# Hybrid decoder trunk: the 20 columns of dt and forget gate, made by token instead of by feature

## The chip, the cores and the metric

The kernel runs as one program on one core of a Trainium2 chip. The metric is the device time of an execution in microseconds (us); lower is better. The engines are PE (TensorE, matmuls; PEld are its weight loads), DVE (VectorE), ACT (ScalarE), POOL (GpSimd) and SP (SyncE, which here only issues DMAs).

## The reference

Two layers, each of three sub-layers on x of 256 tokens by 1024 features: a SwiGLU feed-forward, a token mixer, a second feed-forward. Each has RMS norms before and after and shift, scale and gate rows made from a conditioning vector. The mixer projects h (256x1024) by w_in into 13 pieces and runs four branches on them. Two narrow pieces matter here, 16 columns of dt and 4 of the forget gate:

```python
rq, rk, rv, rg, pu, sz, sxbc, sdt, fq, fk, fv, ff, gl = jnp.split(h @ w_in, points, axis=-1)
dt = jax.nn.softplus(sdt + dt_bias)            # (256, 16)
log_f = jax.nn.log_sigmoid(ff + b_forget)      # (256, 4)
```

dt and its cumulated decays feed the SSD scan, log_f the forgetting attention. Everything else stays as it was.

## The kernel before

**Precision.** Products are made in fp32r, TensorE's rounded 32-bit type. Each operand is split into a high part (the rounded value) and a low part (what is left), and three products are added up: hi x hi, hi x lo, lo x hi. HH and HL (`h_both`) are the two parts of h, by feature: feature on the partitions, 8 blocks k of 128 features, 256 tokens. WH and WL (`w_hi`, `w_lo`) are those of the weights.

**The stream of weight chunks.** All weights of the big products come as 512 KB chunks in one order over both layers, numbered g. SP loads chunk g into RAW, a ring of 8, once chunk g-8 is used up (`w_used`). ACT copies it into WH, a ring of 7 (`split_to`, L1348). DVE writes the difference into WL over the raw data (L1697); a few chunks of the mixer are split on POOL. PE waits for the low part (`weights`, L744) and multiplies. The order on each engine is written by hand: each engine walks over the chunk index c of the sub-layer, and actions are tied to values of c. DVE's walk is up to 4 chunks ahead of c with its splits, ACT's up to 5.

**The mixer's chunks.** The list MIX (L46) says: "fv" has chunks 0 to 3 (made at the boundary), "dtff" is chunk 4, "pu" 5 to 8, "xbc" 9 to 20, then fq, fk, sz and the gates and branches. Outputs of neighbouring entries go to bank pairs 0-1 and 2-3 of PSUM in turn, and the first chunk of an entry waits until the pair was read out: `freed` (L1257). "dtff" has pair 2-3, and so has the first "xbc" entry, chunk 9.

**The 20 columns.** Chunk 4 holds only 8 blocks of 128x20 weights, loaded as [128, 8, 20] (L650). ACT and DVE split its 160 columns as one flat row. PE makes the result by feature: for each k the weights' 20 columns are stationary and 256 tokens of h move (L1249 to L1253), three matmuls for each k, 24 in all, into 20 partitions of bank 2. ACT copies 20x256 values to ZF (L1537). Three chunks later, at c = 7, PE transposes them in two halves of 128 tokens to bank 3 (L1096 to L1100), and DVE at c = 8 reads them by token, adds the bias and makes z and |z| (L2102 to L2109). `z_ok` then frees the pair for chunk 9 and starts ACT's exp at c = 9. At c = 10 DVE makes softplus and the decays from it, which PE needs at c = 16.

Of the kernel before, what the change touches and what calls it, by code (L numbers as in the profile page):

```python
# [14 lines left out]
P = 128  # L15
D = 1024
# [301 lines left out]
def build(nc, x_d, c_d, w_ada, b_ada, norm_pre, norm_post, w_ffn_in, w_ffn_out, w_in, pool_w, w_ret_out, w_pool_out,  # L318
          w_ssm_out, w_fox_out, w_out, vecs_d, consts_d, out_d):
    with ExitStack() as ctx:  # L320
# [47 lines left out]
        EPS = SMALL[:, 16:17]  # L368
        DUMMY = SMALL[:, 17:18]
        _, dg_off = sb("rows_area", [P, TT, P])  # L370
        ZF = at("dt_by_feature", [P, T], F32, dg_off)
        AR = at("decay_rows", [P, T], F32R, dg_off)
        SEL, _ = sb("row_selector", [P, 20], F32R)
        RB = SMALL[:, 18:20]
# [73 lines left out]
        def quad(b):  # L448

            return PS[:, b:b + 2, :].rearrange("p b (h i) -> p (b h) i", h=2)  # L450

        def con(a, n):
            return KC[:, a:a + n]
# [76 lines left out]
        yph_ok = Signal(sem("y_pool_hi_ready"), 1)  # L530
        ypl_ok = Signal(sem("y_pool_lo_ready"), 1)
        pm_ok = Signal(sem("pool_weights_landed"), 16)
        zf_ok = Signal(sem("dt_by_feature_ready"), 1)
        zt_ps = Signal(sem("dt_by_token_in_psum"), 1)
        z_ok = Signal(sem("z_abs_ready"), 1)
        aexp_ok = Signal(sem("a_exp_ready"), 1)
        e_ok = Signal(sem("exp_abs_ready"), 1)
# [203 lines left out]
        def _(pe):  # L741
# [351 lines left out]

            def mixer_core(layer, c):

                if c == 7:  # L1096
                    pe.wait_ge(zf_ok.sem, zf_ok.at(layer, 1))
                    for tt in range(TT):
                        ins = pe.transpose(PS[:, 3, tt * 20:(tt + 1) * 20], ZF[0:20, tok(tt)], ident[0:20, 0:20])
                    ins.then_inc(zt_ps.sem, 1)  # L1100
                if c == 16:
                    if layer == 0:
                        pe.wait_ge(small_landed, 16 * N_SMALL)
# [127 lines left out]
            def mixer(s):  # L1231
                layer = s // 3
                first_tokens(s)

                acts = {"ret": (YRH, YRL, yrl_ok), "pool": (YPH, YPL, ypl_ok),
                        "ssm": (YSH, YSL, ysl_ok), "fox": (YFH, YFL, yfl_ok)}
                freed = [None, None]
                n_gate, n_mul, n_pool, n_sz, n_xbc = 0, 0, 0, 0, 0
                for i, (name, col, n, by_token) in enumerate(MIX):
                    if name == "fv":  # L1240
                        continue
                    pair = i % 2
                    for j in range(n):
                        c = MIX_AT[i] + j
                        g = BASE[s] + c
                        mixer_core(layer, c)
                        if name == "dtff":
                            wh, wl = weights(g)
                            for k in range(KD):  # L1249
                                cs = slice(20 * k, 20 * k + 20)  # L1250
                                mm(PS[0:20, 2, 0:T], wh[:, cs], HH[:, k, :], start=(k == 0), stop=False)
                                mm(PS[0:20, 2, 0:T], wh[:, cs], HL[:, k, :], start=False, stop=False)
                                ins = mm(PS[0:20, 2, 0:T], wl[:, cs], HH[:, k, :], start=False, stop=(k == KD - 1))  # L1253
                            ins.then_inc(w_used, 1)
                            freed[pair] = (z_ok, 1)
                            continue
                        if j == 0 and freed[pair] is not None:  # L1257
                            sig, count = freed[pair]
                            pe.wait_ge(sig.sem, sig.at(layer, count))
                        if by_token:  # L1260
                            hi, lo = HH, HL
                            if name in acts:
                                hi, lo, ready = acts[name]
                                if j == 0 and col == 0:
                                    pe.wait_ge(ready.sem, ready.at(layer, 1))
                            token_chunk(g, j, 2 * pair, hi, lo, 2 * n, (0, 1)).then_inc(w_used, 1)
                            continue
                        wh, wl = weights(g)
                        for kk in range(2):
                            k = 2 * j + kk  # L1270
                            for t in range(4):
                                out = PS[:, 2 * pair + t // 2, (t % 2) * T:(t % 2 + 1) * T]
                                cs = slice(kk * HALF + t * P, kk * HALF + (t + 1) * P)
                                mm(out, wh[:, cs], HH[:, k, :], start=(k == 0 and t % 2 == 0), stop=False)  # L1274
                                mm(out, wh[:, cs], HL[:, k, :], start=False, stop=False)  # L1275
                                ins = mm(out, wl[:, cs], HH[:, k, :], start=False, stop=(k == KD - 1 and t % 2 == 1))  # L1276
                        ins.then_inc(w_used, 1)
                    if name == "gate":
                        n_gate += 1
                        freed[pair] = (gate_ok, n_gate)  # L1280
                    elif name == "pool":
                        n_pool += 1
                        freed[pair] = (pooled_out, n_pool)
                    elif name in ("ssm", "fox", "ret"):
                        n_mul += 1
                        freed[pair] = (gmul_ok, n_mul)
                    elif name == "xbc":
                        n_xbc += 1
                        freed[pair] = (conv_ok, n_xbc)
                    elif name == "sz":  # L1290
                        n_sz += 1
                        freed[pair] = (sz_ok, n_sz)
                    elif name in ("rq", "rk"):
                        freed[pair] = (rcos_ok, 1 if name == "rq" else 2)
                    elif name != "dtff":
                        freed[pair] = ({"pu": pu_ok, "fq": fq_ok, "fk": fk_ok, "rv": rv_ok, "rg": rg_ok}[name], 1)

                def before(k):
                    mixer_core(layer, WOUT + k)
                    if k == 0 and s + 1 < SUBS:  # L1300
                        pe.wait_ge(sh_ok.sem, sh_ok.at(s, 1))
                    if k % 4 == 0:
                        pe.wait_ge(ml_ok.sem, ml_ok.at(layer, k // 4 + 1))

                out_chunks(s, WOUT, KD, YSH, YSL, before)
# [29 lines left out]
        def _(act):  # L1335
# [3 lines left out]
            def split_to(g):  # L1339

                while state["next"] <= min(g, CHUNKS - 1):
                    n = state["next"]
                    state["next"] += 1
                    act.wait_ge(landed[n % N_RAW], LANDED[n])
                    if n >= N_HI:
                        act.wait_ge(w_used, n - N_HI + 1)
                    width = KD * 20 if is_dtff(n) else D
                    fn(WH[:, n % N_HI, 0:width], RAW[:, n % N_RAW, 0:width], ACT.Copy).then_inc(w_hi, 1)  # L1348

            def done(g):  # L1350
                act.wait_ge(w_used, g)
# [168 lines left out]
            def mixer(s):  # L1520
                layer = s // 3
                n_gate, n_sz, n_xbc = 0, 0, 0
                for c in range(N_MIX - TAIL):
                    g = BASE[s] + c
                    ended = [i for i, m in enumerate(MIX) if MIX_AT[i] + m[2] == c]
                    if ended:
# [5 lines left out]
                        if name == "fv":  # L1532
                            done(g)
                            fn(FV[:], PS[:, 6:8, :], ACT.Copy).then_inc(fv_ok.sem, 1)
                        if name == "dtff":
                            done(g)
                            fn(ZF[0:20, :], PS[0:20, 2, 0:T], ACT.Copy).then_inc(zf_ok.sem, 1)  # L1537
                        if name in ("pu", "fq", "fk"):
                            done(g)
                            dst, sig = {"pu": (PU, pu_ok), "fq": (FQ, fq_ok), "fk": (FK, fk_ok)}[name]  # L1540
# [143 lines left out]
        def _(dve):  # L1684
# [3 lines left out]
            def split_to(g):  # L1688

                while state["next"] <= min(g, CHUNKS - 1):  # L1690
                    n = state["next"]
                    state["next"] += 1
                    if splits_on_pool(n):
                        continue
                    dve.wait_ge(w_hi, n + 1)
                    width = KD * 20 if is_dtff(n) else D
                    dve.tensor_tensor(WL[:, n % N_RAW, 0:width], RAW[:, n % N_RAW, 0:width], WH[:, n % N_HI, 0:width],  # L1697
                                      ALU.subtract).then_inc(w_lo, 1)

            def done(g):  # L1700
                dve.wait_ge(w_used, g)
# [345 lines left out]
            def mixer(s):  # L2047
# [3 lines left out]
                for c in range(N_MIX - TAIL):  # L2051
# [47 lines left out]
                        ada_step(t, i)  # L2099
                    if c == 3:  # L2100
                        gate_row(s)
                    if c == 8:  # L2102
                        dve.wait_ge(zt_ps.sem, zt_ps.at(layer, 1))
                        if layer == 0:
                            dve.wait_ge(small_landed, 16 * N_SMALL)
                        chain(dve.tensor_tensor(Z20[:], PS[:, 3, 0:40].rearrange("p (t n) -> p t n", t=2),
                                                vec(layer, V_B20, 20).unsqueeze(1).to_broadcast([P, 2, 20]), ALU.add))
                        chain(dve.tensor_scalar(Z20[:, :, 0:16], Z20[:, :, 0:16], -1.0, None, ALU.mult))
                        dve.scalar_tensor_tensor(E20[:], Z20[:], -1.0, Z20[:], ALU.mult, ALU.max).then_inc(z_ok.sem, 1)  # L2109
                    if c == 10:  # L2110
# [178 lines left out]
        def _(pool):  # L2289
            chain = Order(pool, pool_order)  # L2290

            def split(g):

                if g >= CHUNKS:
                    return
                pool.wait_ge(w_hi, g + 1)
                width = KD * 20 if is_dtff(g) else D
                pool.tensor_tensor(WL[:, g % N_RAW, 0:width], RAW[:, g % N_RAW, 0:width], WH[:, g % N_HI, 0:width],
                                   ALU.subtract).then_inc(w_lo_pool, 1)

            def zero(t, n):
                pool.memset(part(n), 0.0).then_inc(acc_zero.sem, 1)
# [87 lines left out]
```

## Time and profile before

| | us |
|---|---|
| median of 3 runs | 1488.42 (1487.47 to 1488.42) |
| profiled execution, device time | 1487.86 |
| its span, first to last instruction | 1485.8 |
| PE busy | 1473.5 (99%) |
| DVE busy | 1161.1 (78%) |
| ACT busy | 816.5 (55%) |

The span is what the trace covers; the device time is 2.06 us longer. Busy PE says that matmuls were in flight, which overlap: their durations (276 ns for 256 moving columns) are longer than the distance from one start to the next. The distances have to be read from a timeline or from the chain of waits. Times in the rows are us from the span's start unless they are means, which are ns.

### The profile page before, as it was taken

Reading aid. Unit: us, or ns where it says so; the run is one execution under the profiler, and the core shown is the slowest. Engines: PE = TensorE matmul, PEld = TensorE weight load, DVE = VectorE, ACT = ScalarE, POOL = GpSimd, SP = SyncE. Lnnn points to the kernel's source line nnn. Section 1 sums busy time; section 2 is a strip of 40 time slices with the busy share of each in tenths; the row PEclk is TensorE's granted clock in tenths of the full one; section 3 lists DMA queues with packets and bytes.
Section 4 is the critical chain, followed back from the end, with each engine's and each line's share of the span. In section 5 each row is a group of like instructions: output and inputs, shape, how many; then the busy total and the mean of one; then the engine's idle time right before and its main releaser. Section 6 shows DMA issues by size and latency. Waiting matters only on the chain.

```text
span 1485.8 us, 20504 instructions
## 1 busy us (share of the span) xinstructions
PE 1473.5 (99%) x7991; PEld 1259.6 (85%) x7991; DVE 1161.1 (78%) x1414; ACT 816.5 (55%) x1016; POOL 56.8 (4%) x56
## 2 busy tenths in 40 slices
PE   8999999999999999999999999999999999999998
PEld 5788889997988878888888888899888888888886
DVE  6888777867799878889787897776879988775663
ACT  4545465566563456556465564654746545664553
POOL 0000003200000000000000000050000000000000
PEclk9999999999999999999999999999999999999999
DMA  9899966556777847888768887665667787566652
GB/s 349 292 323 303 336 221 206 167 164 186 226 250 245 284 156 241 259 277 286 241 227 263 272 280 250 192 184 158 183 192 244 244 263 234 179 187 186 195 187 99
DMA packets 203623, 342.94 MB, mean 231 GB/s; under 512 B 18547, under 2 KB 118131, under 8 KB 203526
## 3 DMA queue, kind: packets, MB, share of 16 engines
q1 hardware_dynamic: 185382, 275.56, 58.2%
q10 hardware_dynamic: 18144, 66.07, 13.4%
q8 instruction: 63, 1.03, 0.3%
q14 instruction: 34, 0.28, 0.1%
HBM read 340.53 MB, written 1.05 MB: 230 GB/s over the span
## 4 chain that ended last, share of the span: by engine, by line
PE 97%; DVE 2%; ACT 1%; issue 1%; DMA 0%; DVEq 0%; ACTq 0%
PE ps L819 12%; PE ps L784 11%; PE ps L775 11%; PE ps L785 11%; PE ps L933 6%; PE ps L935 6%; PE ps L934 6%; PE ps L824 6%; PE ps L1274 5%; PE ps L1275 5%; PE ps L1276 5%; PE ps L867 3%; PE ps L973 1%; PE ps L860 1%; PE ps L1146 1%
## 5 line engine op out<-in xcount | busy, mean ns | idle before, releaser
L1697 DVE TENSOR_TENSOR w_lo<-w_raw,w_hi 128x1024 fp32r<-128x1024 f32 x480 | 574.7, 1219 | 100.7 <-ACT w_hi L1348 100.2
L1348 ACT ACTIVATE w_hi<-w_raw 128x1024 fp32r<-128x1024 f32 x490 | 504.7, 1051 | 259.5 <-DMA w_raw<-in_w_ffn_out 70.5
L784 PE MATMUL ps<-w_hi,h_both 128*128 128x512 f32 x586 | 231.0, 394 | 0.0
L785 PE MATMUL ps<-w_lo,h_both 128*128 128x512 f32 x586 | 228.3, 390 | 0.0
L775 PE MATMUL ps<-w_hi,h_both 128*128 128x512 f32 x586 | 227.6, 390 | 0.0
L819 PE MATMUL ps<-h_both,w_hi 128*128 128x512 f32 x768 | 206.6, 394 | 0.0
L1274 PE MATMUL ps<-h_both,w_hi 128*128 128x256 f32 x640 | 182.6, 285 | 0.0
L1276 PE MATMUL ps<-h_both,w_lo 128*128 128x256 f32 x640 | 181.1, 283 | 0.0
L1275 PE MATMUL ps<-h_both,w_hi 128*128 128x256 f32 x640 | 181.1, 283 | 0.0
L1713 DVE SCALAR_TENSOR_TENSOR ada_acc<-ada_slab,c_silu,ada_acc 128x1024 f32<-128x1024 f32 x128 | 163.7, 1279 | 5.7 <-DMA ada_slab<-in_w_ada 5.7
L819 PEld LDWEIGHTS ps<-h_both,w_hi 128*128 128x128 f32 x768 | 132.9, 189 | 19.2
L933 PE MATMUL ps<-w_hi,act_hi 128*128 128x512 f32 x352 | 137.6, 391 | 0.0
L935 PE MATMUL ps<-w_hi,act_lo 128*128 128x512 f32 x352 | 137.0, 389 | 0.0
L934 PE MATMUL ps<-w_lo,act_hi 128*128 128x512 f32 x352 | 137.0, 389 | 0.0
L784 PEld LDWEIGHTS ps<-w_hi,h_both 128*128 128x128 f32 x586 | 110.1, 188 | 24.1 <-DVE w_lo L1697 2.4
L775 PEld LDWEIGHTS ps<-w_hi,h_both 128*128 128x128 f32 x586 | 110.0, 188 | 23.4
L785 PEld LDWEIGHTS ps<-w_lo,h_both 128*128 128x128 f32 x586 | 110.2, 188 | 21.8
L824 PEld LDWEIGHTS ps<-h_both,w_lo 128*128 128x128 f32 x768 | 114.5, 189 | 14.2
L1274 PEld LDWEIGHTS ps<-h_both,w_hi 128*128 128x128 f32 x640 | 122.7, 192 | 0.6 <-issue 0.3
L1275 PEld LDWEIGHTS ps<-h_both,w_hi 128*128 128x128 f32 x640 | 122.8, 192 | 0.2
L1276 PEld LDWEIGHTS ps<-h_both,w_lo 128*128 128x128 f32 x640 | 122.7, 192 | 0.0
L824 PE MATMUL ps<-h_both,w_lo 128*128 128x256 f32 x768 | 118.3, 281 | 0.0
(310 smaller groups left out, 1860.2 us busy)
## 6 DMA issues: line engine op xcount, KB each, us to landing
w_raw<-in_w_ffn_in SPq DMA_DIRECT2D x352, 256.0 KB, 3.8
w_raw<-in_w_in SPq DMA_DIRECT2D x168, 512.0 KB, 3.7
ada_slab<-in_w_ada ACTq DMA_DIRECT2D x126, 512.0 KB, 4.6
w_raw<-in_w_ffn_out SPq DMA_DIRECT2D x88, 512.0 KB, 4.2
w_raw<-in_w_ssm_out SPq DMA_DIRECT2D x16, 512.0 KB, 4.7
w_raw<-in_w_out SPq DMA_DIRECT2D x16, 512.0 KB, 3.4
ada_slab_first<-in_w_ada SPq DMA_DIRECT2D x14, 512.0 KB, 7.2
w_raw<-in_w_pool_out SPq DMA_DIRECT2D x8, 512.0 KB, 3.6
```

The costliest lines, as they stand in the source:

```text
L775: return mm(PS[:, banks + tt, :], lo[:, k, tok(tt)], wh[:, kk * HALF:(kk + 1) * HALF], start=False, stop=(k == kn - 1))
L784: mm(out, hi[:, k, tok(tt)], wh[:, cs], start=(k == 0), stop=False)
L785: mm(out, hi[:, k, tok(tt)], wl[:, cs], start=False, stop=False)
L819: ins = mm(PS[:, bank, :], wh[:, cs], HB[:, k, :, :], start=(k == 0), stop=(k == KD - 1))
L824: ins = mm(PS[:, bank, 0:T], wl[:, cs], HH[:, k, :], start=False, stop=False)
L933: mm(out, hi[:, k, tok(tt)], wh[:, cs], start=first, stop=False)
L934: mm(out, hi[:, k, tok(tt)], wl[:, cs], start=False, stop=False)
L1274: mm(out, wh[:, cs], HH[:, k, :], start=(k == 0 and t % 2 == 0), stop=False)
L1275: mm(out, wh[:, cs], HL[:, k, :], start=False, stop=False)
L1276: ins = mm(out, wl[:, cs], HH[:, k, :], start=False, stop=(k == KD - 1 and t % 2 == 1))
L1348: fn(WH[:, n % N_HI, 0:width], RAW[:, n % N_RAW, 0:width], ACT.Copy).then_inc(w_hi, 1)
L1697: dve.tensor_tensor(WL[:, n % N_RAW, 0:width], RAW[:, n % N_RAW, 0:width], WH[:, n % N_HI, 0:width], ALU.subtract).then_inc(w_lo, 1)
```

## The change

h becomes the stationary operand and the weights move. For each half of 128 tokens and each k, the 128x128 tile of HH is loaded and the 40 columns [hi | lo] of the weights move through it; then the tile of HL is loaded and the 20 hi columns move. That makes 32 matmuls, and the result stands by token: for half tt, columns 64 tt to 64 tt + 19 of bank 2 hold the products with the hi weights, the next 20 those with the lo weights. The copy to ZF and the two transposes go. DVE reads at c = 7 (it waits for the chunk's last matmul), with one more add that joins the two groups of 20. The hi and lo weights stand side by side in one buffer of WH, in runs of 20 columns.

```diff
+        def dt_weights(g):
+            return WH[:, g % N_HI, 0:KD * 40].rearrange("p (k n) -> p k n", k=KD)
+        def dt_raw(g):
+            return RAW[:, g % N_RAW, 0:KD * 20].rearrange("p (k n) -> p k n", k=KD)
...
             def mixer_core(layer, c):
-                if c == 7:
-                    pe.wait_ge(zf_ok.sem, zf_ok.at(layer, 1))
-                    for tt in range(TT):
-                        ins = pe.transpose(PS[:, 3, tt * 20:(tt + 1) * 20], ZF[0:20, tok(tt)], ident[0:20, 0:20])
-                    ins.then_inc(zt_ps.sem, 1)
...
                         if name == "dtff":
-                            wh, wl = weights(g)
-                            for k in range(KD):
-                                cs = slice(20 * k, 20 * k + 20)
-                                mm(PS[0:20, 2, 0:T], wh[:, cs], HH[:, k, :], start=(k == 0), stop=False)
-                                mm(PS[0:20, 2, 0:T], wh[:, cs], HL[:, k, :], start=False, stop=False)
-                                ins = mm(PS[0:20, 2, 0:T], wl[:, cs], HH[:, k, :], start=False, stop=(k == KD - 1))
+                            weights(g)
+                            both = dt_weights(g)
+                            for tt in range(TT):
+                                for k in range(KD):
+                                    mm(PS[:, 2, tt * SHD:tt * SHD + 40], HH[:, k, tok(tt)], both[:, k, :],
+                                       start=(tt == 0 and k == 0), stop=False)
+                                    ins = mm(PS[:, 2, tt * SHD:tt * SHD + 20], HL[:, k, tok(tt)], both[:, k, 0:20], start=False,
+                                             stop=(tt == TT - 1 and k == KD - 1))
                             ins.then_inc(w_used, 1)
...
# ACT
-                    width = KD * 20 if is_dtff(n) else D
-                    fn(WH[:, n % N_HI, 0:width], RAW[:, n % N_RAW, 0:width], ACT.Copy).then_inc(w_hi, 1)
+                    if is_dtff(n):
+                        fn(dt_weights(n)[:, :, 0:20], dt_raw(n), ACT.Copy).then_inc(w_hi, 1)
+                        continue
+                    fn(WH[:, n % N_HI, :], RAW[:, n % N_RAW, :], ACT.Copy).then_inc(w_hi, 1)
...
-                        if name == "dtff":
-                            done(g)
-                            fn(ZF[0:20, :], PS[0:20, 2, 0:T], ACT.Copy).then_inc(zf_ok.sem, 1)
...
# DVE
+                    if is_dtff(n):
+                        dve.tensor_tensor(dt_weights(n)[:, :, 20:40], dt_raw(n), dt_weights(n)[:, :, 0:20], ALU.subtract)\
+                            .then_inc(w_lo, 1)
+                        continue
...
-                    if c == 8:
-                        dve.wait_ge(zt_ps.sem, zt_ps.at(layer, 1))
+                    if c == 7:
+                        done(BASE[s] + at_unit("dtff") + 1)
                         if layer == 0:
                             dve.wait_ge(small_landed, 16 * N_SMALL)
-                        chain(dve.tensor_tensor(Z20[:], PS[:, 3, 0:40].rearrange("p (t n) -> p t n", t=2),
-                                                vec(layer, V_B20, 20).unsqueeze(1).to_broadcast([P, 2, 20]), ALU.add))
+                        z = PS[:, 2, 0:2 * SHD].rearrange("p (t n) -> p t n", t=2)
+                        chain(dve.tensor_tensor(Z20[:], z[:, :, 0:20], vec(layer, V_B20, 20).unsqueeze(1).to_broadcast([P, 2, 20]),
+                                                ALU.add))
+                        chain(dve.tensor_tensor(Z20[:], z[:, :, 20:40], Z20[:], ALU.add))
                         chain(dve.tensor_scalar(Z20[:, :, 0:16], Z20[:, :, 0:16], -1.0, None, ALU.mult))
                         dve.scalar_tensor_tensor(E20[:], Z20[:], -1.0, Z20[:], ALU.mult, ALU.max).then_inc(z_ok.sem, 1)
```

## Rows read from the trace of the kernel before

**Rows 1.** The page: busy time by engine; the ended-last chain by engine.

```profile
PE 1473.5 (99%) x7991; PEld 1259.6 (85%) x7991; DVE 1161.1 (78%) x1414; ACT 816.5 (55%) x1016; POOL 56.8 (4%) x56
...
PE 97%; DVE 2%; ACT 1%; issue 1%; DMA 0%; DVEq 0%; ACTq 0%
```

**Rows 2.** Waits of PE (who waited for what: us in total, times, longest).

```profile
PE ps L1317 <- ACT c_silu L1668: 3.4, 1, 3.4
PE ps L984 <- DVE ada_acc_hi L1905: 1.8, 2, 0.9
PE ps L759 <- ACT h_both L1423: 0.5, 1, 0.5
PE ps L860 <- DVE act_full L1927: 0.3, 1, 0.3
```

**Rows 3.** Chain around the chunk: start us, us, what. Layer 1, then layer 0.

```profile
957.45 0.12 PE ps L1251
...
960.08 0.11 PE ps L1253
960.20 0.12 PE ps L1274
...
965.83 0.12 PE ps L1276
965.95 0.23 PE ps L1099 x2
966.18 0.32 PE ps L1274
...
231.21 0.12 PE ps L1251
...
233.96 0.12 PE ps L1274
...
239.59 0.12 PE ps L1276
239.71 0.23 PE ps L1099 x2
239.94 0.32 PE ps L1274
```

**Rows 4.** Timeline of weight loads: start us, us, engine, line (x: merged count).

```profile
413.06 0.64 PEld L1181 LDWEIGHTS ps<-small_columns,squares_ssd 128*128 128x128 f32 x4
413.62 0.19 PEld L784 LDWEIGHTS ps<-w_hi,h_both 128*128 128x128 f32 x1
...
266.55 0.30 PEld L1108 LDWEIGHTS ps<-da,consts 128*128 128x128 f32 x2 [0.17 <-issue]
266.76 0.30 PEld L1109 LDWEIGHTS ps<-da,consts 128*128 128x128 f32 x2
266.99 0.19 PEld L1274 LDWEIGHTS ps<-h_both,w_hi 128*128 128x128 f32 x1
...
337.54 0.53 PEld L1082 LDWEIGHTS ps<-decay_rows,row_selector 128*128 128x128 f32 x4 [0.17 <-issue]
```

**Rows 5.** The transposes: timeline of PE, then groups by form (busy, mean ns).

```profile
239.64 0.30 PE L1099 MATMUL ps<-consts,dt_by_feature 20*128 20x20 f32 x2
...
L1099 PE MATMUL ps<-consts,dt_by_feature 20*128 20x20 f32 x4 | 0.6, 222 | 0.0
```

**Rows 6.** Groups by form, DVE and ACT: busy us, mean ns of one.

```profile
L1697 DVE TENSOR_TENSOR w_lo<-w_raw,w_hi 128x160 fp32r<-128x160 f32 x2 | 0.6, 320 | 0.0
...
L1537 ACT ACTIVATE dt_by_feature<-ps 20x256 f32<-20x256 f32 x2 | 0.7, 364 | 0.3 <-PE ps L1253 0.3
L1348 ACT ACTIVATE w_hi<-w_raw 128x160 fp32r<-128x160 f32 x2 | 0.7, 330 | 0.0
```

**Rows 7.** Timeline of layer 1: start us, us, engine, line.

```profile
954.12 4.86 DVE L1697 TENSOR_TENSOR w_lo<-w_raw,w_hi 128x1024 fp32r<-128x1024 f32 x5
...
957.06 0.10 PEld L1251 LDWEIGHTS ps<-h_both,w_hi 128*20 128x20 f32 x1
...
960.02 3.49 DVE L1697 TENSOR_TENSOR w_lo<-w_raw,w_hi 128x1024 fp32r<-128x1024 f32 x3
...
964.12 1.23 DVE L1697 TENSOR_TENSOR w_lo<-w_raw,w_hi 128x1024 fp32r<-128x1024 f32 x1 [0.61 <-ACT w_hi L1348]
...
966.64 1.23 DVE L1697 TENSOR_TENSOR w_lo<-w_raw,w_hi 128x1024 fp32r<-128x1024 f32 x1 [1.30 <-ACT w_hi L1348]
```

**Rows 8.** Timeline of DVE, layer 0, with the z group.

```profile
233.80 4.80 DVE L1697 TENSOR_TENSOR w_lo<-w_raw,w_hi 128x1024 fp32r<-128x1024 f32 x4
239.79 1.23 DVE L1697 TENSOR_TENSOR w_lo<-w_raw,w_hi 128x1024 fp32r<-128x1024 f32 x1 [1.19 <-ACT w_hi L1348]
240.93 0.19 DVE L2106 TENSOR_TENSOR z<-ps,vectors 128x40 f32<-128x40 f32 x1
241.16 0.18 DVE L2108 TENSOR_SCALAR z<-z 128x32 f32<-128x32 f32 x1
241.37 0.20 DVE L2109 SCALAR_TENSOR_TENSOR e<-z 128x40 f32<-128x40 f32 x1
```

**Rows 9.** Start: chain; then windows of PE (busy, granted clock, DMA share, GB/s).

```profile
3.37 3.75 PE ps L1317 x4
7.12 3.71 PE ps L1312 x8
...
15.22 1.31 PE ps L1312 x6
...
0.00:15.00 15.00, 11.63 (x23) 1.00 0.91 299
...
957.00:960.20 3.20, 3.20 (x28) 1.00 1.00 323
```

**Rows 10.** Timeline of PE around the 16 transposes of XBC.

```profile
290.13 1.91 PE L1118 MATMUL ps<-consts,xbc 128*128 128x128 f32 x16
291.80 0.36 PE L1274 MATMUL ps<-h_both,w_hi 128*128 128x256 f32 x1
292.00 0.28 PE L1275 MATMUL ps<-h_both,w_hi 128*128 128x256 f32 x1
292.12 0.28 PE L1276 MATMUL ps<-h_both,w_lo 128*128 128x256 f32 x1
```

More of the change, by code:

```diff
@@ L370, in build @@
         _, dg_off = sb("rows_area", [P, TT, P])
-        ZF = at("dt_by_feature", [P, T], F32, dg_off)
         AR = at("decay_rows", [P, T], F32R, dg_off)
@@ L532, in build @@
         pm_ok = Signal(sem("pool_weights_landed"), 16)
-        zf_ok = Signal(sem("dt_by_feature_ready"), 1)
-        zt_ps = Signal(sem("dt_by_token_in_psum"), 1)
         z_ok = Signal(sem("z_abs_ready"), 1)
@@ L1695, in split_to @@
                     dve.wait_ge(w_hi, n + 1)
-                    width = KD * 20 if is_dtff(n) else D
-                    dve.tensor_tensor(WL[:, n % N_RAW, 0:width], RAW[:, n % N_RAW, 0:width], WH[:, n % N_HI, 0:width],
-                                      ALU.subtract).then_inc(w_lo, 1)
+                    if is_dtff(n):
+                        dve.tensor_tensor(dt_weights(n)[:, :, 20:40], dt_raw(n), dt_weights(n)[:, :, 0:20], ALU.subtract)\
+                            .then_inc(w_lo, 1)
+                        continue
+                    dve.tensor_tensor(WL[:, n % N_RAW, :], RAW[:, n % N_RAW, :], WH[:, n % N_HI, :], ALU.subtract)\
+                        .then_inc(w_lo, 1)
             def done(g):
@@ L2296, in split @@
                 pool.wait_ge(w_hi, g + 1)
-                width = KD * 20 if is_dtff(g) else D
-                pool.tensor_tensor(WL[:, g % N_RAW, 0:width], RAW[:, g % N_RAW, 0:width], WH[:, g % N_HI, 0:width],
-                                   ALU.subtract).then_inc(w_lo_pool, 1)
+                pool.tensor_tensor(WL[:, g % N_RAW, :], RAW[:, g % N_RAW, :], WH[:, g % N_HI, :], ALU.subtract)\
+                    .then_inc(w_lo_pool, 1)
             def zero(t, n):
```

## The prediction

> **What bounds the kernel now.** I read the page first. TensorE (PE) is busy for 1473.5 of 1485.8 us, and 97% of the chain that ended last is PE [rows 1]. The waits of PE's own instructions come next: apart from one wait of 3.4 us at the very start they are 1.8, 0.5 and 0.3 us in the whole run [rows 2]. So each us that PE issues more or less moves the end by a us, and what VectorE (DVE), ScalarE (ACT) and the DMA queue do counts only if PE begins to wait for it. Then the chain of waits around the 20-column chunk, once per layer (at 231 us and at 957 us). It is PE alone: 24 matmuls of the chunk, then the chunks of "pu", with two transposes three chunks later [rows 3]. The change touches these two stretches of PE and little else.
>
> **What goes from PE.** The 24 matmuls of a layer (L1251 to L1253, 20 stationary columns, 256 moving) run from 957.45 to 960.20, which is 2.75 us, 115 ns each; in layer 0 from 231.21 to 233.96, also 2.75 us [rows 3]. The two transposes at L1099 and the matmul behind them last from 965.95 to 966.50 (0.23 + 0.32), where a matmul of this stream takes 0.12. They cost 0.43 us; in layer 0, from 239.71 to 240.25, 0.42 us [rows 3]. Together 3.17 us per layer.
>
> **What comes to PE.** Two token halves by eight k give 16 pairs: a 128x128 stationary tile of h hi with 40 moving columns, and one of h lo with 20. That is 32 weight loads of 128 columns and only 960 moving columns, where 6,144 moved before. The moving columns can hardly be the price: at the 115 ns of 256 columns [rows 3] 40 of them are 18 ns. The load is. No row has a rounded (fp32r) matmul with under 256 moving columns, so I take the price from loads that stand close together. Four loads of 128x128 with one moving column (L1181): the first is issued at 413.06 under the matmul before; their group lasts 0.64, so the last began at 413.51, and the next line's load at 413.62, 0.11 later [rows 4]. Two with 20 moving columns at L1108 start at 266.55, two at L1109 at 266.76, and the next line's load at 266.99: 0.44 us for four, 110 ns each [rows 4]. Four rounded loads with a broadcast stationary (L1082): (0.53 - 0.19) / 3 = 113 ns [rows 4]. I take 110 ns: 32 x 0.110 = 3.52 us.
>
> Upwards: with 256 moving columns beside a full load the pace is 120 ns (960.20 to 965.95, 48 matmuls) [rows 3]; that gives 3.84 us. Further up, if a load did not run beside the matmul before it, 110 ns and the moving columns would add, 18 and 9 ns at the rate above: 32 x 0.1235 = 3.95 us. Furthest, if short rounded matmuls took as long as 256 columns and the loads added to that: 32 x (0.115 + 0.110) = 7.2 us; I give that end little, since every stream in the rows overlaps the two. Downwards: the two transposes of 20 columns with a quick load (their busy times 0.30 together, 0.222 for one) follow each other after 80 ns [rows 5]; 32 x 0.08 = 2.56 us. Two short loads or a load of another mode are no load of 128 rounded columns, so 110 is the nearer.
>
> Whether load and matmul overlap can be read: at the 120 ns pace [rows 3] there is no room for a full load of 110 ns and 256 moving columns one after the other. The Trainium skill speaks against the change here. "TensorE: Matmul & The Clock Gate", section "Part 3: Packing small matmuls", says that a load overlaps running matmuls only when they use other row groups; by it 128 full rows make load and matmul serial, 3.95 us per layer. The trace disagrees with its pace of 120 ns, and the trace decides.
>
> **PE's sum.** Per layer +3.52 - 2.75 - 0.42 = +0.35 us; two layers +0.70 us. Bounds: -1.22 us with the 80 ns pace (2.56 - 3.17 = -0.61 per layer), +1.34 with 120 ns, +1.56 with serial loads, +8.1 at the far end.
>
> **The waits.** PE's chunk still waits for the low part. The two copies and subtractions of 160 columns, now written in runs of 20 into one buffer, took 330 and 320 ns [rows 6]; the DVE group with it began at 954.12, behind one full subtraction of 1.22 it ends about 955.7, and PE's first load of the chunk starts at 957.06 [rows 7]. 1.4 us of slack cover a strided access even at double time. The first user of the other bank pair (the first "xbc" chunk, which waits for z_ok) begins after four "pu" chunks of 24 matmuls, 2.9 us each: about 972 in layer 1, and z_ok comes near 966.
>
> DVE gets one more 40-column add (about 0.19 us) and the group of z moves ahead of the subtraction of chunk 12. It is four instructions instead of three, 0.64 us from the first's start to the last's end, and 0.23 more for the new one: 0.87 us [rows 8]. In layer 1 chunk 11's subtraction ends at 965.35 and chunk 12's starts at 966.64, when ACT's copy is there: 1.29 us of idle time, of which 0.87 are used. In layer 0 the four subtractions end at 238.60 and the next starts at 239.79: 1.19 us [rows 7, 8]. The new wait in front (for the chunk's last matmul, about 961 and 235) is then long over; behind it is only chunk 12, which PE reads some 15 us later. Without that cover the price would be 0.87 us of DVE, not of PE. ACT loses a copy of 0.36 us [rows 6] and the stop before it; SP asks for chunk 12 some 0.77 us later, because the dt chunk is used up later, and PE is as late itself. All of that I put at nothing, and between -0.3 and +0.3 us.
>
> **From the sum to the time.** The profiled execution took 1487.86 us for its span of 1485.8. Plus 0.70 it would be 1488.56. The median of the runs shown, 1488.42, lies 0.56 above the profiled one, and the runs lie between 1487.47 and 1488.42; on the median the change makes 1489.1 us, which is what I predict.
>
> **The rivals.**
>
> 1. The loads come quicker than 110 ns. PE has only 20 or 40 columns between them, and the quickest neighbours in the trace are 80 ns apart [rows 5]. For it: less than a fifth of the moving columns. Against it: the three groups at 110 and 113 ns, one of them with a single moving column [rows 4]. It gives -1.22 us: 1487.2. The Trainium skill's page on TensorE, section "Back-to-back issue gap", has about 81 ns for a sustained stream with 128 columns; by that figure as an estimate the new block would be 2.6 us.
>
> 2. The load is not hidden, or a short rounded matmul has a floor of its own: +1.3 to +1.6 us from the two upper prices, 1489.7 to 1490.0, and in its tail up to +8.1, 1496.5. Against it stands the single-column group again.
>
> 3. The clock, which is the case on the slower side. The new block is the longest stretch in which the array mostly waits for loads, 3.5 us with 960 columns. At the start of the kernel 8 matmuls of 512 columns took 3.71 us (464 ns each, the pace of the 1.2 GHz level, though the granted clock is given as 1.00), and 6 of them later 1.31 us (218 ns, 2.4 GHz); PE had waited 3.4 us before [rows 2, 9]. If PE fell back to that pace after the new block, the same stretch would lose 3.71 - 8 x 0.218 = 2.0 us per layer, and if the four matmuls ahead of it (3.75 us) were slowed by half too, up to 3.9 us. Total +0.70 + 4.0 to 7.8: 1493.1 to 1496.9. It decides from 1.1 us lost per layer on. Against it: 16 transposes of 128x128 from 290.13 to 291.80 are followed by matmuls 0.12 us apart [rows 10], and the granted clock is 1.00 in every stretch [rows 9]. The same page of the Trainium skill, section "Part 1: The HAM clock gate", says that the clock is granted by how busy the array has lately been; by it a thin stream is a risk. No row has 3.5 us of such a stream.
>
> **Chances.** The forecast (load pace near 110 ns, PE's sum passed to the end) 0.72; rival 1 0.13; rival 2 0.09, a fifth of it beyond 0.2%; rival 3 0.03; unknown effects of moved instructions and buffers 0.03. About 0.2%, 3.0 us, is what a measurement here can tell from no change: 1485.4 to 1491.4. The forecast, rival 1 and most of rival 2 lie within; so 0.03 faster, 0.91 same, 0.06 slower. The range goes from rival 1 less the scatter of the runs (about 1 us) to rival 2 with it: 1486.2 to 1491.2.
>
> **What would show it.** Right: the 32 loads of the new block 107 to 115 ns apart; the block about 3.5 us from its first matmul to the first of "pu"; an even 0.12 us pace at chunk 7, where the transposes were; DVE's z group between chunks 11 and 12 with no wait in front; the "pu" matmuls at 0.12 us right after the block. Wrong: loads 80 ns apart or less (rival 1); over 120 ns (rival 2); "pu" matmuls at over 0.2 us behind the block (rival 3); a wait of PE for z or for the low part of the weights, or a change of more than 3 us elsewhere.

## The result and the profile after

| | before | changed |
|---|---|---|
| median, us | 1488.42 | 1491.91 |
| fastest and slowest of 17 runs | 1487.47 to 1489.34 | 1488.78 to 1495.72 |
| profiled execution, device time | 1487.86 | 1494.78 |
| its span | 1485.8 | 1492.8 |

The ratio is 1.0023, 95% interval 1.0016 to 1.0029: slower, by 3.5 us in the median. The forecast was 1489.1 with a range that ended at 1491.2. The spread is part of the result. The runs of before lie within 1.9 us, those of the changed kernel within 6.9. Each run also comes with the mean clock granted to TensorE over its span: the 7 runs of 1488.78 to 1489.98 have 0.999 or 1.000, the 10 of 1491.64 to 1495.72 have 0.995 to 0.998.

The page of the changed kernel, to be read against [rows 1]:

```profile
PE 1479.3 (99%) x8003; PEld 1265.5 (85%) x8003; DVE 1161.5 (78%) x1416; ACT 815.4 (55%) x1014; POOL 56.8 (4%) x56
```

PE is busy 5.8 us longer, for 12 matmuls more. Its own waits (us in total, times, longest) are 7.1 us, where those of [rows 2] are 6.0:

```profile
PE ps L1319 <- ACT c_silu L1669: 3.3, 1, 3.3
PE ps L989 <- DVE ada_acc_hi L1909: 2.5, 3, 0.9
PE ps L764 <- ACT h_both L1427: 0.5, 1, 0.5
...
PE ps L978 <- DVE y_tok L1849: 0.3, 1, 0.3
```

Three short waits are new. Those of L1013 (0.16 us, at 14.1) and the third of L989 (0.78 us, at 173.7) lie ahead of the first new block, and no other profile has them. That of L978 (0.26 us, at 1306.4) is in the profile of every kernel that starts from the changed one (their transposes of `y_tok`, under other line numbers), and not in those of before, e4 and e6; what brings it is not shown. Most of the 7.0 us of span is something else: PE became slower while it was busy. The windows of PE around the two blocks show where (stretch in us, its length, PE busy and matmuls, granted clock, DMA share, GB/s):

```profile
232.20:235.30 3.10, 3.10 (x30) 1.00 1.01 305
235.30:242.10 6.80, 6.80 (x34) 0.51 0.58 202
242.10:252.00 9.90, 9.90 (x84) 0.99 0.70 192
...
961.90:965.80 3.90, 3.90 (x36) 1.00 0.99 321
965.80:969.30 3.50, 3.50 (x19) 0.51 0.86 296
969.30:980.00 10.70, 10.70 (x91) 1.00 0.64 178
```

In both layers the clock is at 1.00 (2.4 GHz) through all or most of the new block and then at half, 1.2 GHz, for 6.8 us in layer 0 and 3.5 us in layer 1. I call that a fall. The chain of waits shows where it sets in and the pace, for layer 0 and then layer 1 (start us, us, what; L1252 has 40 moving columns, L1254 has 20, L1276 to L1278 are the "pu" matmuls that stood at L1274 to L1276 before):

```profile
232.43 0.02 PE ps L1252
...
232.56 0.12 PE ps L1252
232.68 0.10 PE ps L1254
...
235.46 0.18 PE ps L1252
235.64 0.20 PE ps L1254
235.84 0.23 PE ps L1252
236.08 0.20 PE ps L1254
236.27 0.41 PE ps L1276
236.68 0.21 PE ps L1277
...
242.02 0.21 PE ps L1278
242.23 0.16 PE ps L1276
242.39 0.12 PE ps L1277
...
962.18 0.02 PE ps L1252
...
965.65 0.22 PE ps L1276
...
966.02 0.21 PE ps L1278
...
969.41 0.12 PE ps L1276
```

In layer 0 the block begins at 232.43 and its last four matmuls, from 235.46 on, are slow. In layer 1 the whole block, 962.18 to 965.65, is at full pace, and the fall comes right behind it. A pair of the block takes 0.22 us, in layer 0's slow end 0.43. The "pu" matmuls behind it are 0.21 us apart, where [rows 3] has 0.12, until 242.2 (in layer 1 until 969.2); then 0.12 is back, with nothing changed in what PE does. The weight loads (start us, us) show the block's pace, 111 ns from load to load, and 213 once the clock has gone:

```profile
233.05 0.19 PEld L1252 LDWEIGHTS ps<-w_hi,h_both 128*128 128x128 f32 x1
233.16 0.19 PEld L1254 LDWEIGHTS ps<-w_hi,h_both 128*128 128x128 f32 x1
...
235.41 0.34 PEld L1254 LDWEIGHTS ps<-w_hi,h_both 128*128 128x128 f32 x1
235.62 0.34 PEld L1252 LDWEIGHTS ps<-w_hi,h_both 128*128 128x128 f32 x1
```

DVE, layer 0, beside [rows 8] (start us, us, engine, line):

```profile
235.02 4.62 DVE L1701 TENSOR_TENSOR w_lo<-w_raw,w_hi 128x1024 fp32r<-128x1024 f32 x4
239.56 0.20 DVE L2111 TENSOR_TENSOR z<-ps,vectors 128x40 f32<-128x40 f32 x1
239.79 0.20 DVE L2113 TENSOR_TENSOR z<-ps,z 128x40 f32<-128x40 f32 x1
240.02 0.18 DVE L2114 TENSOR_SCALAR z<-z 128x32 f32<-128x32 f32 x1
240.24 0.20 DVE L2115 SCALAR_TENSOR_TENSOR e<-z 128x40 f32<-128x40 f32 x1
242.78 1.23 DVE L1701 TENSOR_TENSOR w_lo<-w_raw,w_hi 128x1024 fp32r<-128x1024 f32 x1 [2.34 <-ACT w_hi L1352]
```

The z group of four starts right after the four subtractions, with no wait, and is done 2.3 us before the next subtraction can start. The block of layer 0 begins at 232.4 us, where the old one began at 231.2. That is not the start of the kernel: at PE's wait for `act_full`, at 59.7 us, the two executions are still level. 0.8 us of the 1.2 are the wait at 173.7.

### The profile page after: what moved, and what is told of

Its sections match the earlier page's. It is cut to its first block, busy times and chain, and to the rows that moved or that the text cites. A ratio compares the mean times of both kernels' runs of the same rounds, so it can differ in the third digit from the quotient of the medians.

```text
span 1492.8 us, 20528 instructions
## 1 busy us (share of the span) xinstructions
PE 1479.3 (99%) x8003; PEld 1265.5 (85%) x8003; DVE 1161.5 (78%) x1416; ACT 815.4 (55%) x1014; POOL 56.8 (4%) x56
## 4 chain that ended last, share of the span: by engine, by line
PE 86%; DVE 2%; DMA 0%; issue 0%; ACT 0%; ACTq 0%; DVEq 0%
PE ps L824 12%; PE ps L789 8%; PE ps L780 8%; PE ps L790 8%; PE ps L829 6%; PE ps L938 6%; PE ps L940 6%; PE ps L939 6%; PE ps L1276 5%; PE ps L1278 5%; PE ps L1277 5%; PE ps L872 3%; PE ps L978 1%; PE ps L1146 1%; DVE w_lo L1701 0%; DMA ada_slab<-in_w_ada 0%
## 5 line engine op out<-in xcount | busy, mean ns | idle before, releaser
L1276 PE MATMUL ps<-h_both,w_hi 128*128 128x256 f32 x640 | 184.5, 288 | 0.0
L1278 PE MATMUL ps<-h_both,w_lo 128*128 128x256 f32 x640 | 183.0, 286 | 0.0
L1277 PE MATMUL ps<-h_both,w_hi 128*128 128x256 f32 x640 | 182.9, 286 | 0.0
L824 PEld LDWEIGHTS ps<-h_both,w_hi 128*128 128x128 f32 x768 | 133.0, 189 | 19.1
L1276 PEld LDWEIGHTS ps<-h_both,w_hi 128*128 128x128 f32 x640 | 124.9, 195 | 0.5 <-issue 0.3
L1277 PEld LDWEIGHTS ps<-h_both,w_hi 128*128 128x128 f32 x640 | 124.8, 195 | 0.2
L1278 PEld LDWEIGHTS ps<-h_both,w_lo 128*128 128x128 f32 x640 | 124.7, 195 | 0.0
```

What stands on the lines that cost most here:

```text
L824: ins = mm(PS[:, bank, :], wh[:, cs], HB[:, k, :, :], start=(k == 0), stop=(k == KD - 1))
```

## The experiments

All but e4 and e6 start from the changed kernel. "Before" is the kernel before on the same chip in the same job: 1488.71 for e1 to e4, 1488.03 for e5 to e7, 1488.73 for e8 and e9 (medians). Each job has its own. The changed kernel itself was not in the job of e1 to e4; there e4 is the run that shows the fall.

**e1: more columns through the same loads.**

```diff
-mm(PS[:, 2, tt * SHD:tt * SHD + 40], HH[:, k, tok(tt)], both[:, k, :], ...)
-mm(PS[:, 2, tt * SHD:tt * SHD + 20], HL[:, k, tok(tt)], both[:, k, 0:20], ...)
+mm(PS[:, 2, tt * T:tt * T + 128], HH[:, k, tok(tt)], flat[:, 40 * k:40 * k + 128], ...)
+mm(PS[:, 2, tt * T:tt * T + 128], HL[:, k, tok(tt)], flat[:, 40 * k:40 * k + 128], ...)
```

> The changed kernel with 128 moving columns in each of its 32 matmuls of the dt chunk (columns behind the 40 or 20 wanted ones are read from the same buffer and not used; z reads 256 columns apart). Loads, order and waits are the same. Theory (the few moving columns let the granted clock fall): the loads still set a pace near 0.111 us, the block stays at 3.5 to 3.7 us, but the clock holds 1.00 and the 'pu' matmuls behind it stay 0.12 us apart: 1488.7 to 1489.5, and no run near 1492 or 1495. Rival (it is the closely spaced 128-column loads, or the block's length, whatever moves through): the clock falls as in the changed kernel, 1491 to 1495.

Measured: 1489.26 (1488.70 to 1491.24, 11 runs), ratio 1.0005 (0.9997 to 1.0014). No run has a mean clock under 0.999. The windows of its block and of what follows:

```profile
232.00:235.80 3.80, 3.80 (x36) 1.00 1.01 292
235.80:242.00 6.20, 6.20 (x53) 1.00 0.80 276
```

36 matmuls in the first window, as many as a block at full clock needs, and 53 in the second at 1.00, where the changed kernel had 34 matmuls in 6.8 us. Four times the columns cost no time, and no fall shows. One reservation: the short fall of layer 1 takes only 0.001 off the mean of a run, so one could hide in a mean rounded to 0.999; of e1's runs that is open for the one at 1491.24, and that run has no trace. The loads, their spacing and the block's length are those of the changed kernel, so they alone do not bring the fall: how little moves through matters.

**e2: the same 32 matmuls in two halves.**

```diff
+if name == "pu" and j == 0 and kk == 1 and t == 3:
+    dt_half(1).then_inc(w_used, 1)      # the second 128 tokens, behind 21 "pu" matmuls
...
-for tt in range(TT):                    # at the dt chunk
-    ...
+dt_half(0)
```

> The changed kernel with its 32 matmuls in two halves: the 16 of the first 128 tokens where they were, the 16 of the second 128 behind 21 of the first 'pu' chunk's 24 matmuls, 2.5 us later. Same instructions in total. Theory (one stretch of 3.5 us with few columns is what lowers the clock): no fall, 1488.7 to 1489.5 in every run, the sum of the prediction. Rival (the number of thin matmuls counts, however placed): the clock falls in part of the runs and the median is above 1490.5.

Measured: 1489.42 (1488.81 to 1490.19, 11 runs), ratio 1.0004 (0.9995 to 1.0013), no run with a mean clock under 0.999; the five at 0.999 are not above 1489.02, so none of them hides a fall. Placement alone removes the fall. The instructions and their pace are those of the changed kernel, so this is what the change costs with the clock held: +0.7 us.

**e3 and e9: by feature, with the parts side by side.**

```diff
-for tt in range(TT):
-    ...
+for k in range(KD):                     # in the last k the two change places
+    mm(PS[0:40, 2, 0:T], both[:, k, :], HH[:, k, :], start=(k == 0), stop=False)
+    mm(PS[0:20, 2, 0:T], both[:, k, 0:20], HL[:, k, :], start=False, stop=False)
...
+fn(ZF[0:40, :], PS[0:40, 2, 0:T], ACT.Copy).then_inc(zf_ok.sem, 1)
...
+ins = pe.transpose(PS[:, 3, tt * SHD:tt * SHD + 40], ZF[0:40, tok(tt)], ident[0:40, 0:40])
```

> The dt chunk by feature again, with hi and lo weights side by side as 40 stationary columns: 8 matmuls of [hi | lo] on h hi and 8 of hi on h lo, 256 moving columns each, 16 instead of 24; ACT copies 40 rows, two transposes of 40x128, DVE adds the two groups of 20. Theory: PE's pace is set by moving columns, 115 ns each, so 1.84 us instead of 2.75 per layer, and the transposes cost 0.43 as before: -0.9 us per layer, -1.8 us against the kernel before, 1486.6, and the clock holds. Rival (16 short matmuls cost more with 40 stationary columns, or what PE gives free is lost to a wait behind it): no gain, 1488.4.

> e3_feature40 once more, beside e8_hidden12: 1486.3 to 1487.2 in most runs, 0.1% under the kernel before and about 1 us under e8_hidden12; clock held.

Measured: 1486.74 (1486.34 to 1488.25, 11 runs) and 1487.13 (1486.28 to 1488.19, 11 runs), each time ratio 0.9989 (0.9980 to 0.9998); -2.0 and -1.6 us on their before. This beats both kernels. The chain of e3:

```profile
231.19 0.12 PE ps L1260
...
232.69 0.23 PE ps L1261 x2
232.92 0.12 PE ps L1263
```

From 231.19 to 232.92 plus one matmul: 16 in 1.85 us, 115 ns each. With 40 stationary columns the pace is that of 20, and eight matmuls per layer are saved: 0.9 us, as expected.

**e4 and e6: the block alone, in the kernel before.**

```diff
 wh, wl = weights(g)
+if c == 6:
+    for m in range(16):                 # 8 in e6
+        tt, mk = m // 8, m % 8
+        mm(PS[:, 3, 128:168], HH[:, mk, tok(tt)], wh[:, 0:40], start=(m == 0), stop=False)
+        mm(PS[:, 3, 128:148], HL[:, mk, tok(tt)], wh[:, 0:20], start=False, stop=(m == 15))
```

> The kernel before, with 32 extra matmuls added (16 pairs of a 128x128 stationary tile with 40 and with 20 moving columns, output not used) ahead of chunk 6 of each mixer. This is the changed kernel's block alone, with nothing else of the change. Theory: each block costs 32 x 0.111 = 3.55 us and lets the clock fall: 7.1 us without a fall (1495.5), 8.7 to 13.5 with falls in one or both layers, the median between 1497 and 1502. Rival (the fall comes from something else of the change, such as the moved z group or the copies): 1495.5 in every run, clock 1.00 behind the block.

> The kernel before with a block of 16 thin matmuls (8 pairs of 40 and 20 moving columns, output not used) ahead of chunk 6 of each mixer, half of the block of e4_added16. Theory (the length of the thin stretch decides): the clock holds; 2 x 16 x 0.111 = +3.6 us over the kernel before, 1492.3, in every run within 1 us. Rival (thin matmuls let the clock fall at any length): some runs 2 us or more higher, median over 1493.5.

Measured, e4: 1498.31 (1497.75 to 1501.55, 5 runs), ratio 1.0069 (1.0056 to 1.0081). 7.1 us for the blocks would be 1495.8; every run is at least 1.9 us above, with a mean clock of 0.998 or 0.996. In the profiled one layer 0 fell, right behind the block (237.62 to 241.10), and layer 1 did not:

```profile
236.00:240.00 4.00, 4.00 (x38) 1.00 0.89 293
240.00:244.00 4.00, 4.00 (x24) 0.63 0.20 74
...
968.00:972.00 4.00, 4.00 (x38) 1.00 0.90 289
```

e6: 1491.92 (1491.13 to 1492.61, 10 runs), ratio 1.0024 (1.0015 to 1.0033); +3.9 us against the 3.6 expected, no clock under 0.999. The block brings the fall along with nothing else of the change, and half of it in a row did not in any of ten runs.

**e5: the changed kernel again.**

> The changed kernel once more, beside the others on one chip. Theory (in each layer's block the clock falls or not, by chance, at 2 to 3 us a fall): the times lie in three groups, near 1489.1 (no fall), 1491.9 (one) and 1494.6 (two), with at least one run in two of the groups. Rival (a single slower level with noise): the times spread evenly around 1491.9.

Measured: 6 runs from 1488.71 to 1489.54 with clocks of 0.999 or 1.000; 1492.39, 1492.58 and 1492.79 with 0.997 or 0.998; 1494.18 and 1495.38 with 0.996. Nothing lies between 1489.54 and 1492.39. Of one level with noise that would be odd. Ratio 1.0017 (1.0007 to 1.0027). The profiled run took 1492.79 and fell in layer 1 only:

```profile
232.00:235.80 3.80, 3.80 (x36) 1.00 0.94 320
235.80:242.00 6.20, 6.20 (x54) 1.00 0.71 242
...
961.80:965.50 3.70, 3.70 (x18) 0.50 0.88 299
```

The chain of layer 1 has the start of the block and the place where the pace changes, 2.6 us later:

```profile
958.56 0.02 PE ps L1252
...
961.14 0.18 PE ps L1252
```

Layer 0 of the same execution has the block with the clock held (chain of waits):

```profile
231.89 0.02 PE ps L1252
...
235.26 0.10 PE ps L1254
235.37 0.22 PE ps L1276
235.59 0.12 PE ps L1277
```

The block takes 3.48 us, and the first "pu" matmul 0.22 instead of 0.12: 3.58 us. With the first 17 runs, the changed kernel fell in 15 of 28. The other 13 have a median of 1488.96.

**e7: 64 columns.** The edit of e1 with 64 in place of 128.

> The changed kernel with 64 moving columns in each of its 32 matmuls, between the changed kernel's 30 on average and e1_wide128's 128. Same loads, order and waits. Theory (columns moved per time decide): twice the columns of the changed kernel lower the clock less often, so that the median lies at or under 1491 and over half of the runs are near 1489.2. Rival (only near-full streams hold it): falls as often as in the changed kernel, median 1491.5 to 1495.

Measured: seven runs from 1488.96 to 1489.87 at a clock of 0.999 or 1.000, four from 1492.67 to 1494.75 at 0.996 to 0.998. Ratio 1.0017 (1.0009 to 1.0026). 4 falls in 11 against 15 in 28 is too few to call it rarer; against e1's none in 11 it is some evidence that more columns help.

**e8: 12 of the 32 among wide matmuls.**

```diff
 for k in (2 * j, 2 * j + 1):            # last "fv" chunk, 512 columns each
     first_product(0, k, HH, wl, stop=(k == KD - 1))
+    dt_pair(j, k % 2)                   # two thin ones; the same behind the next four
```

> The changed kernel with 12 of its 32 thin matmuls placed among the last six 512-column matmuls of the 'fv' chunks, two behind four of them and four behind the fifth; 20 stay where they were. Theory (a load runs beside the matmul before it, so a stretch costs the larger of its loads at 0.111 us and its columns): the six wide and twelve thin ones take 18 x 0.111 = 2.0 us instead of 6 x 0.228 + 12 x 0.111 = 2.7, -0.7 us per layer, 1487.7, and with 20 in a row (2.2 us) the clock holds. Rival (load and matmul are serial with full rows, or thin matmuls cost 0.111 us each wherever they are): 1489.1. Rival (the clock falls with fewer too): some runs 2 us or more above the rest.

Measured: 1491.41 (1488.76 to 1494.78, 11 runs), ratio 1.0020 (1.0011 to 1.0029). Six runs from 1488.76 to 1491.41 have a clock of 0.999 or 1.000, five from 1492.24 on have 0.996 to 0.998. The expectation failed twice. PE's timeline (L872 is a wide matmul, L927 and L928 are the thin ones):

```profile
231.44 0.48 PE L872 MATMUL ps<-w_lo,h_both 128*128 128x512 f32 x1
231.75 0.18 PE L927 MATMUL ps<-w_hi,h_both 128*128 128x40 f32 x1
231.78 0.26 PE L928 MATMUL ps<-w_hi,h_both 128*128 128x20 f32 x1
231.89 0.47 PE L872 MATMUL ps<-w_lo,h_both 128*128 128x512 f32 x1
232.20 0.18 PE L927 MATMUL ps<-w_hi,h_both 128*128 128x40 f32 x1
```

From one wide matmul to the next it is 0.45 us, as much as the 0.228 of a wide one and twice the 0.111 of a thin one. Nothing is hidden. Three loads of 0.111 would fit within 0.33, but the second and third don't run ahead under the wide matmul. That fits a price per matmul of the larger of its own columns and the next one's load. And the clock falls with 12 thin ones among wide ones and 20 in a row as well. (In the profiled run, clock held, it is 5.07 us from the first of these wide matmuls to the second "pu" matmul; the same stretch of the kernel before takes 4.22. That is +0.85 for the layer, as in the changed kernel with its 3.58 for 2.75; the median of those six runs, 1490.5, is 1.8 us above its before. About 1 us of that is not explained; that job's before itself reaches 1490.35, and the run at 1491.41, with 0.999, could hold a short fall.)

## Why the prediction was wrong

**What held.** PE bounds the kernel, and what PE issues is what is paid. The old block was 2.75 us per layer and the transposes 0.43. The new block was forecast at 3.52 us from 110 ns per load; it measures 111 ns per load and 3.58 us. The sum of +0.70 us for both layers is what the runs with the clock held show: the 7 of the first 17 have a median of 1489.22, +0.8 us on 1488.42; the 6 of e5 +0.9 on their before; e2 +0.7, e1 +0.6. The covers held too: z waits for nothing, and ACT's and DVE's strided 160 columns take 328 and 318 ns. One later wait of PE did appear, the 0.26 us at L978, within the 0.3 us that the prediction allowed for such effects.

**What failed** is rival 3, "the clock", and its chance of 0.03. Its mechanism and price were in the prediction: a fall behind the new block, "up to 3.9 us" per layer, 1493.1 to 1496.9 in total if both layers fall. Both fell in the profiled run, at 1494.78. That this lies within the forecast of rival 3 is in part luck: the two falls cost 4.5 us, near the low end of its 4.0 to 7.8, and 1.2 us came ahead of the first block. The step that failed is the one that put the time behind the new block at nothing: the sum holds no term for the clock, where the profiled run lost 3.0 us in layer 0 and 1.5 in layer 1. The error is in the evidence set against it. The 16 transposes of [rows 10] last 1.7 us, half of the new block, and e6 now shows that half a block is harmless; they could not speak for 3.5 us. The granted clock of 1.00 in [rows 9] was that of stretches in which many columns moved, and in the first 15 us it stands beside matmuls at 464 ns, so that there it shows nothing. The prediction itself said that no row has 3.5 us of such a stream, and still gave 0.03. A case that no row covers should have had the chance of an open question. 15 runs in 28 fell, at +3 to +7 us, and the median is that of whichever kind has the majority: 10 of the first 17 fell, so it is 1491.91, a fallen run, while in e5 5 of 11 fell and it is 1489.54, a held one, inside the range. The range ended at 1491.2, since rival 3 was left out of it.

The price of a fall: at half clock a "pu" matmul takes 0.213 us instead of 0.120. With the clock held, the block and its first "pu" matmul take 3.70 us (e5's layer 0) and each further one 0.12. In layer 0 the block and 28 "pu" matmuls should take 6.9 us and took 10.0 (232.43 to 242.39): 3.0 lost. In layer 1 the block and 18 of them should take 5.7 and took 7.2 (962.18 to 969.41): 1.5 lost. So a fall has two sizes here. The 7.0 us of span are then 4.5 for the two falls, 0.8 for the longer blocks, 1.2 ahead of the first block and 0.3 for the wait at L978, 6.8 in all. e5's profiled run, at 1492.79, has one fall, of the long kind: 3.0 us. The other runs have no trace, so how many falls each had is not shown.

The granted clock falls to 0.51 in a stretch in which the profile lists PE as busy 100% of the time. The rule about the clock, "TensorE: Matmul & The Clock Gate", section "Part 1: The HAM clock gate" of the Trainium skill, says that the clock follows how busy the array has been. By the profile's busy share the trace does not agree with it; it can agree only if that rule's busy is something else than the share of time with a matmul in flight, and e1 (more columns, no fall) points that way. No run shows what the chip counts. The rule on loads that I set aside, that a load overlaps only with matmuls in other row groups (section "Part 3: Packing small matmuls"), is not borne out by this case: e1's block, with 128 columns per matmul, keeps the pace of the block with 30 on average, 111 ns from load to load, so the two do overlap.

**Rival 1**, quicker loads, and **rival 2**, loads that are not hidden, are both refuted by the 111 ns, and so is the estimate of 2.6 us for the block that stood beside rival 1: e1 has 128 moving columns and takes 3.5 us. That the change does less work for PE was never so: the weights that had 20 columns to load now have 128, and PE pays for the larger of load and columns.

What stays open is what makes one execution fall and the next one not, and what makes a fall long or short; no experiment varied that. e1 and e2 show which blocks did not fall, not how the chip decides. Other places for the second half of e2 were not tried.

## What to carry to other kernels

Price a matmul of such a stream by the larger of its moving columns and the next stationary load, one load ahead and no more (e1 and e8). Turning 256 moving columns over 20 stationary ones into 40 moving over 128 is no saving, while putting two narrow stationary operands side by side is one (e3). And a row of thin matmuls of some us is a risk of its own: look at the granted clock behind it over several runs, break it up, or let more columns run through, which cost nothing in e1, where the load took longer than the 128 columns.

## What the runs showed of the hardware that was not expected

- With PE busy all the time, the granted clock went to half 2.6 us (e5), 3.0 us (layer 0) and 3.5 us (layer 1) after the block's start, and stayed there for 6.8 us in one layer and 3.5 in the other, although the full "pu" stream had followed.
- Whether it falls differs from run to run of one program: 15 of 28 for 32 thin matmuls in a row, 5 of 5 in e4, 5 of 11 in e8, 4 of 11 with 64 columns, none of 11 with 128 columns (one run of them open) or in two halves, none of 10 with 16 in a row.
- A wide matmul followed by two thin ones takes 0.45 us, the plain sum of 0.228 and twice 0.111 (e8).
- 20 or 40 stationary columns make no difference beside 256 moving ones: 115 ns both times.
